# Gate products behind the next mixer tile, and the last sums of squares taken later, in a two-block transformer on one core

## The reference

```python
# second block; h: 1040 tokens (16 meta tokens ahead) x 1024
u = rmsnorm_2(h, g_pre_mix[l])
z = u @ w_in[l]                      # 512 q, 128 k, 128 v, 512 xr, 512 yr
...
xr = causal_depthwise_conv(xr, conv_w[l], conv_b[l])        # width 4
# rg_lru: block-diagonal gates, 8 blocks of 64
r = sigmoid(xb @ w_a + b_a);  i = sigmoid(xb @ w_x + b_x)
a = exp(-8 * r * softplus(-lam))
u = sqrt(-expm1(2 * log_a)) * (i * x)
h_t = a_t * h_(t-1) + u_t                                   # over the tokens
rec = gelu(yr) * hr
mix = concatenate([attn, rec]) @ w_out[l]
h = h + rmsnorm_2(mix, g_post_mix[l])
u = rmsnorm_2(h, g_pre_ffn[l])
f = square(relu(u @ w_ff1[l])) @ w_ff2[l]                   # 1024 -> 4096 -> 1024
h = h + rmsnorm_2(f, g_post_ffn[l])
return h[:, N_META:]
```

## Time and profile before

| | |
|---|---|
| device time, median of 3 runs | 2332.53 us (2332.31 to 2332.61) |
| device time of the profiled execution | 2331.14 us, its span 2329.0 us |
| mean granted PE clock of it | 0.953 |
| PE busy | 2198.0 us, 94% |
| DVE busy | 1763.4 us, 76% |
| ACT busy | 1131.9 us, 49% |
| POOL busy | 421.9 us, 18% |

### The profile page before, as it was taken

One profiled execution on the slowest core, in us unless ns is written; L12 is line 12 of the kernel. 1 busy time (PEld: TensorE's weight loads), 2 busy tenths in 40 slices (PEclk: granted clock), 3 DMA queues, 4 the chain that ended last, 5 costly groups with the idle time before them and its releaser, 6 DMA issues. The chain is left out here.

```text
span 2329.0 us, 31104 instructions
## 1 busy us (share of the span) xinstructions
PE 2198.0 (94%) x10909; PEld 1868.8 (80%) x10909; DVE 1763.4 (76%) x2938; ACT 1131.9 (49%) x1944; POOL 421.9 (18%) x417
## 2 busy tenths in 40 slices
PE   8989899998999999999999989899999999999996
PEld 5779888886877788888887979777878788888875
DVE  7699855565599987878788585573799977767897
ACT  5478655554353333335444563484563333554442
POOL 2123122213330122220001212103321122000002
PEclk9985599999999999999999999899999999999997
DMA  9025200005443333238531101002356445755422
GB/s 380 29 71 154 79 14 14 32 1 169 150 136 119 142 115 115 90 118 315 186 93 40 46 28 37 19 2 97 103 190 239 168 153 195 246 197 179 124 91 73
DMA packets 93098, 276.38 MB, mean 119 GB/s; under 512 B 11137, under 2 KB 15649, under 8 KB 89121
## 3 DMA queue, kind: packets, MB, share of 16 engines
q1 hardware_dynamic: 85472, 226.64, 29.3%
q10 hardware_dynamic: 7488, 47.98, 5.0%
HBM read 208.19 MB, written 66.39 MB: 118 GB/s over the span
## 5 line engine op out<-in xcount | busy, mean ns | idle before, releaser
L159 PE MATMUL banks<-f_hi,f_w_hi 128*128 128x512 f32 x608 | 237.8, 391 | 5.8 <-DVE f_w_lo L3914 4.4
L160 PE MATMUL banks<-f_lo,f_w_hi 128*128 128x512 f32 x608 | 237.3, 390 | 0.0
L161 PE MATMUL banks<-f_hi,f_w_lo 128*128 128x512 f32 x608 | 237.2, 390 | 0.0
L3442 ACT CAST f_w_hi<-f_raw 128x512 fp32r<-128x512 f32 x173 | 107.5, 622 | 255.3 <-PE banks L161 190.3
L2017 ACT CAST w_hi<-w_raw 128x512 fp32r<-128x512 f32 x152 | 93.8, 622 | 223.7 <-PE set L161 106.5
L159 PE MATMUL set<-gate_hi,w_hi 128*128 128x512 f32 x420 | 163.8, 390 | 1.2 <-DVE w_lo L2349 0.8
L161 PE MATMUL set<-gate_hi,w_lo 128*128 128x512 f32 x420 | 163.4, 389 | 0.0
L160 PE MATMUL set<-gate_lo,w_hi 128*128 128x512 f32 x420 | 163.4, 389 | 0.0
L159 PE MATMUL set<-b_hi,w_hi 128*128 128x512 f32 x384 | 150.3, 391 | 4.8 <-ACT work L2027 2.6
L3122 POOL TENSOR_TENSOR f_w_lo<-f_raw,f_w_hi 128x512 fp32r<-128x512 f32 x64 | 93.6, 1464 | 337.6 <-ACT f_w_hi L3442 337.6
L161 PE MATMUL set<-b_hi,w_lo 128*128 128x512 f32 x384 | 149.5, 389 | 0.0
(11 more groups left out here) (583 smaller groups left out, 6093.9 us busy)
## 6 DMA issues: line engine op xcount, KB each, us to landing
gates<-x ACTq DMA_DIRECT2D x25, 1536.0 KB, 6.0
w_raw<-in_w_ff SPq DMA_DIRECT2D x53, 512.0 KB, 3.7
gate_raw<-gates SPq DMA_DIRECT2D x105, 256.0 KB, 2.9
f_gate_raw<-gates SPq DMA_DIRECT2D x70, 256.0 KB, 2.8
ada<-in_ada_w SPq DMA_DIRECT2D x32, 512.0 KB, 3.5
f_raw<-in_f_w_v SPq DMA_DIRECT2D x26, 512.0 KB, 3.6
f_raw<-in_f_w_u SPq DMA_DIRECT2D x25, 512.0 KB, 3.8
down_raw<-in_w_ff SPq DMA_DIRECT2D x18, 512.0 KB, 5.1
```

The source lines that it names most:

```text
L159: nc.tensor.matmul(out, w_hi, x_hi, start=start, stop=False)
L160: nc.tensor.matmul(out, w_hi, x_lo, start=False, stop=False)
L161: return nc.tensor.matmul(out, w_lo, x_hi, start=False, stop=stop)
L3442: nc.scalar.copy(w_parts(n)[0][:, :], source(n)).then_inc(w_hi_s, 1)
```

## The change

It has three parts, all of them in the written-out lists of steps.

1. **Recurrent half.** PE takes mixer tile 4+t ahead of gate set t. `gated(t)` is cut into `gated_input(t)` and `factor(t)`, and DVE's list is written in a new order; the four `recurred` stand at its end. On ACT, `weights_mix(5)` stands ahead of `conv_hi(0)`, `weights_mix(6)` to `(9)` between `exp_tanh` and `mult_root`, and the four `gelu` behind the last `mult_root`.
2. **Up projection.** `early_out(15)` stands two squares and one cast earlier in ACT's list.
3. **End.** `y_sum` comes one tile later on DVE, `sum_y` two tiles later on PE. POOL adds the squares of tiles 0 to 3 of the last piece to one, in three adds ahead of its residual adds; `sum_last` is done for t = 0 (that sum), 4, 5, 6, 7, the first two of them between the last tiles of products. The last sums get places in two PSUM banks. `spread_y(0)` and `spread_y(1)` are later on PE, and DVE's `scale_y` follow them.

```diff
--- before.py
+++ after.py
@@ -1551,16 +1551,17 @@
                                "y_inverted", "y_spread", "y_scaled"))
+        end_paired = c.sem("end_paired")
...
-        y_spread_at = [up[1][:, 0, 0:512], up[1][:, 1, 0:256], out[0][:, 0, 0:256]]
+        y_spread_at = [up[1][:, 0, 0:512], up[0][:, 1, 0:256], out[0][:, 0, 0:256]]
         end_square = [(end_sq if t < HALF else end_more)[:, t % HALF * 256:(t % HALF + 1) * 256] for t in range(KT)]
-        y_total_at = [up[0][:, 1, 0:4], up[0][:, 1, 4:6],
-                      up[0][:, :, 8:9].rearrange("p a b -> p (a b)")]
+        y_total_at = [up[0][:, 1, 0:4], up[0][:, 1, 4:6]]
+        y_last_at = [up[0][:, 0, 8:9], up[1][:, 1, 256:257]]
...
@@ -1741,6 +1742,12 @@
                         weights_low(n)
+                pool.wait_ge(y_squared, 2 * KT + 2)
+                nc.gpsimd.tensor_tensor(end_square[0], end_square[0], end_square[1], ALU.add).then_inc(end_paired, 1)
+                pool.wait_ge(y_squared, 2 * KT + 4)
+                nc.gpsimd.tensor_tensor(end_square[2], end_square[2], end_square[3], ALU.add).then_inc(end_paired, 1)
+                pool.wait_ge(end_paired, 2)
+                nc.gpsimd.tensor_tensor(end_square[0], end_square[0], end_square[2], ALU.add).then_inc(end_paired, 1)
...
@@ -1897,9 +1904,12 @@
                 def sum_last(t):
-                    pe.wait_ge(y_squared, 2 * KT + t + 1)
+                    if t == 0:
+                        pe.wait_ge(end_paired, 3)
+                    else:
+                        pe.wait_ge(y_squared, 2 * KT + t + 1)
                     for j in range(2):
-                        mm = nc.tensor.matmul(y_total_at[2][:, j:j + 1], end_square[t][:, j * P:(j + 1) * P],
+                        mm = nc.tensor.matmul(y_last_at[j], end_square[t][:, j * P:(j + 1) * P],
...
@@ -1950,15 +1960,17 @@
                     for t in range(KT):
-                        if t == 3:
+                        if q == 2 and t == 4:
+                            spread_y(0)
+                        if t == 5:
                             sum_y(q - 1)
-                        if t == 7:
-                            spread_y(q - 1)
                         last_down(q, t)
-                pe.wait_ge(y_weighed, 2)
-                for t in range(KT):
+                        if q == 2 and t >= 6:
+                            sum_last(0 if t == 6 else HALF)
+                for t in range(HALF + 1, KT):
                     mm = sum_last(t)
                 mm.then_inc(y_total, 1)
+                spread_y(1)
...
@@ -2167,17 +2179,19 @@
                 early_out(13)
-                for k in range(4):
+                weights_high(17)
+                for k in range(2):
                     square_h(k)
-                weights_high(17)
                 early_out(14)
+                square_h(2)
+                early_out(15)
+                square_h(3)
+                weights_high(18)
                 for k in range(4, 6):
                     square_h(k)
-                weights_high(18)
-                early_out(15)
-                square_h(6)
                 weights_high(19)
-                square_h(7)
+                for k in range(6, 8):
+                    square_h(k)
...
@@ -2235,7 +2249,7 @@
                         y_square(q, t)
-                        if t == 4:
+                        if t == 6:
...
@@ -2612,6 +2626,13 @@
 
+                def weigh_last():
+                    dve.wait_ge(y_total, 3)
+                    for j in range(2):
+                        n = cols[2].start + j
+                        op = nc.vector.tensor_tensor(part[:, n:n + 1], y_last_at[j], scale2[:, n:n + 1], ALU.mult)
+                    op.then_inc(y_weighed, 1)
+
...
@@ -2625,33 +2646,32 @@
 
-                last_add(0, 0)
+                for q in range(2):
+                    for t in range(KT):
+                        last_add(q, t)
+                        if t > 1:
+                            y_sum(q, t - 1)
+                        elif t == 0 and q:
+                            y_sum(q - 1, KT - 1)
+                        if q and t == 6:
+                            weigh(0)
+                invert_y(0)
+                last_add(2, 0)
+                y_sum(1, KT - 1)
                 for t in range(1, KT):
-                    last_add(0, t)
-                    y_sum(0, t)
-                for t in range(KT):
-                    last_add(1, t)
-                    if t:
-                        y_sum(1, t)
-                    if t == 3:
-                        weigh(0)
-                    if t == 5:
-                        invert_y(0)
-                for t in range(KT):
                     last_add(2, t)
-                    if t == 3:
+                    if t == 6:
                         weigh(1)
-                    if t == 5:
-                        invert_y(1)
-                    if t % 2:
-                        scale_y(0, t // 2)
-                for k in range(HALF, KT):
+                    if t >= 4:
+                        scale_y(0, t - 4)
+                invert_y(1)
+                for k in range(4, 6):
                     scale_y(0, k)
-                weigh(2)
-                for k in range(HALF):
-                    scale_y(1, k)
+                weigh_last()
+                scale_y(0, 6)
+                scale_y(0, 7)
                 invert_y(2)
-                for k in range(HALF, KT):
+                for k in range(KT):
...
@@ -3404,8 +3424,8 @@
                 for t in range(LRU_T):
+                    mix_products(4 + t)
                     gates_of(t)
-                    mix_products(4 + t)
...
@@ -3769,33 +3789,30 @@
                 nc.scalar.activation(lam_t[3][:, :], lam_t[2][:, :], ACT.Ln, bias=1.0).then_inc(lam_act, 1)
+                weights_mix(5)
                 conv_hi(0)
-                weights_mix(5)
                 sigmoids(0)
                 conv_hi(1)
                 exp_tanh(0)
+                weights_mix(6)
                 mult_root(0)
-                weights_mix(6)
                 sigmoids(1)
                 conv_hi(2)
                 exp_tanh(1)
+                weights_mix(7)
                 mult_root(1)
-                weights_mix(7)
                 sigmoids(2)
                 conv_hi(3)
-                gelu(0)
                 exp_tanh(2)
+                weights_mix(8)
                 mult_root(2)
-                weights_mix(8)
                 sigmoids(3)
-                gelu(1)
                 exp_tanh(3)
+                weights_mix(9)
                 mult_root(3)
-                weights_mix(9)
-                gelu(2)
-                weights_mix(10)
-                gelu(3)
-                for n in (11, 12, 13):
+                for t in range(LRU_T):
+                    gelu(t)
+                for n in (10, 11, 12, 13):
...
@@ -4332,10 +4349,12 @@
 
-                def gated(t):
+                def gated_input(t):
                     dve.wait_ge(gate_free, 2 * CH2 * (t + 1))
                     nc.vector.tensor_tensor(lru.gi[:, :], lru.gi[:, :], lru.xc[t % 2][:, :], ALU.mult)\
                         .then_inc(gated_s, 1)
+
+                def factor(t):
...
@@ -4399,28 +4418,30 @@
                 evacuate(XR[3], work[:, 3, :]).then_inc(xr_used, 1)
+                gate_branch(0)
+                gated_input(0)
                 conv_lo(1)
+                factor(0)
                 rescale(2)
-                gated(0)
                 state(0)
                 convolve_2(2)
-                gate_branch(0)
                 conv_lo(2)
-                gated(1)
+                gated_input(1)
+                factor(1)
+                gate_branch(1)
                 state(1)
                 convolve_2(3)
-                gate_branch(1)
                 conv_lo(3)
-                gated(2)
+                gated_input(2)
+                factor(2)
+                gate_branch(2)
                 state(2)
-                gate_branch(2)
-                recurred(0)
-                gated(3)
+                gated_input(3)
+                factor(3)
+                gate_branch(3)
                 state(3)
-                recurred(1)
-                gate_branch(3)
-                recurred(2)
-                recurred(3)
+                for t in range(LRU_T):
+                    recurred(t)
...
```

## The result

| | before | changed |
|---|---|---|
| device time, median of 5 runs | 2332.61 us (2332.31 to 2333.53) | 2315.11 us (2311.85 to 2320.15) |
| ratio, 95% interval | | 0.9924 [0.9913, 0.9935] |
| span of the profiled execution | 2329.0 | 2313.3 |
| granted PE clock of it | 0.953 | 0.955 |

What follows compares the result with a forecast made beforehand. TensorE (PE), busy 94% of the span, was taken to bound the kernel. Terms of -9.9 (recurrent half), -1.2 (early copy) and -8.0 (end) sum to -19.1, from 2332.5 to 2313.4 us; range 2307 to 2321.

Steps and rivals of the forecast that it cites:

- -9.9: Recurrent half: one whole mixer tile moves into PE's waits, 1.7 us of it lost to a later last gate set.
- -1.2: Up projection: ACT's copy comes 1.7 us earlier, but a low part from DVE then comes 0.6 too late; 1.2 us gained.
- -8.0: End: DVE's last add 8.6 us earlier, its first final add waiting for POOL until 2312.6; DVE ends at 2318.9, not 2326.9.
- PE without a wait at set 0; tile 8 near 1404.7: Recurrent half: gate set 0 starts at 1348.1 without a wait; gate set 3 ends and mixer tile 8 starts near 1404.7.
- No wait at set 1: Recurrent half: a chain of 11.4 us from 1352.2 starts sigmoids 1 at 1363.6, when PE has just reached the set.
- Cycles of 18.5, the second product about 3.2: Recurrent half: state chain 18.5 us for tiles 2 and 3; DVE's second product of each tile about 3.2 beside POOL's subtraction.
- two cycles 1.95 shorter each: Bound for the recurrent half: if POOL never got ahead of DVE's second product, about -13.5 us.
- Waits of 3.5 and 2, and the clock at half in both: Recurrent half: PE waits some 3.5 us in gate set 2 and 2 in set 3, and the granted clock falls there.
- Rival (a): End: DVE is let in between POOL's instructions, end term -12.1, total -23.2, 2309.3 us; chance 0.15.
- (b): Recurrent half: the state chain sets it with its old longest cycle of 21.1, total -13.9, 2318.6 us; chance 0.15.
- (c): Recurrent half: PE loses in sets 2 and 3 what it saves at 0 and 1; total -9.2, 2323.3 us; chance 0.04.
- (d): PE's clock stays at 1.2 GHz through the tile behind sets 1, 2 and 3: +15.5, 2348.0 us; chance 0.03.

Runs made afterwards that it cites:

- later_gates: Changed kernel with gate sets 2 and 3 behind two mixer tiles each, DVE and ACT steps fitted, a one-column sigmoid behind each root: 2309.8 us, ratio 0.9897 to before.
- small_low: Changed kernel with POOL's subtraction for the low weights of mixer tiles 6 to 9 on 128 of 1024 columns: 2312.1 us, ratio 0.9899 to before.
- psum_inverse: Changed kernel with the inverse of the last piece in PSUM: 2317.4 us, ratio 0.9923 to before.
- psum_end: Changed kernel with the inverse of the last piece and the last eight scaled products in PSUM: 2315.8 us, ratio 0.9920 to before.

## Why the prediction was right

The forecast was 2313.4 against 2315.1, within its range. Its three terms were -9.9, -1.2 and -8.0. The recurrent half came as -10.5 in the first trace and as -8.0 to -9.5 in the seven other traces with the same half; the early copy gave nothing (M is 0.3 longer, and 0.2 to 0.5 at the place itself); the end came as -8.7. That the sum of the stretches, -18.9, is so near to -19.1 is in part luck: a larger end and a good draw of the clock in the half stand for the missing -1.2, and the 3.2 of the early part, which no term had, moved the span the other way.

- **PE without a wait at set 0; tile 8 near 1404.7.** Both so: 0.17, and 1404.5 on the scale of before.
- **No wait at set 1.** Wrong by 1.5. My chain from set 0 to sigmoids 1 had the table load follow the root; it waits for PE's first group of the set, 1.16 after the root's end. Sigmoids 1 started at 1368.26, not 1366.8 (1363.6 and the 3.2 by which this execution was late). With the load taken ahead in later_gates the wait was 0.45. The chain also left out `rescale(2)` and the product of the state, but that product ended at 1367.09, before the load was through, and cost nothing here.
- **Cycles of 18.5, the second product about 3.2.** 18.8 (root to root, 1364.73 to 1383.51) and 3.33. small_low shows the cause: with POOL's subtraction cut from 2.52 us to 0.59 the product is 1.39. The bound of "two cycles 1.95 shorter each" was right for the product; A became 1.9 to 4.3 us shorter than in the eight traces.
- **Waits of 3.5 and 2, and the clock at half in both.** 2.62 and 2.57, and behind which set the clock fell changed from one execution to the next, so A lies between 136.8 and 139.2 in eight traces of kernels that are the same in this half. The waits of sets 1 to 3 are 6.7 in sum where 5.5 was forecast, and the clock fell behind one of them instead of two; these errors offset each other in the first trace.
- **-1.2 for the early copy.** The term is wrong, by 1.2 and more. The wait became 1.7 shorter, and the three low parts behind it took back 1.3 (0.56 + 0.43 + 0.29), of which I had counted the first alone (0.6, it was 0.56). The rest went in the products between, in steps too small for the timeline to name: over the whole place it is 17.0 against 16.7.
- **-8.0 for the end.** The mechanism holds, its place was another. I had put POOL's backlog in front of the first final add (4.4 us); it came in front of the two-column product (3.25), then POOL ran dry for 0.49, and the adds got through at 0.69 and less. psum_inverse moves it back to where I had it, 5.31. The terms ahead are as worked out: last add after 14.5 (14.4 forecast). POOL ended 1.6 later than forecast. As forecast, PE stood at no sum of squares.
- Rival (a), DVE let in between POOL's adds, is half true: DVE came in at the next boundary where the operation took 0.94 and 0.69, and was kept out where it took 3.25 and 5.31. Rivals (b) and (c) didn't come, nor did (d), the slow clock through whole tiles: behind the waits of the changed kernel it lasted 3 to 7 us.

What stays open: why DVE comes in at one boundary of POOL's adds and is kept out over seven at another, what decides whether the clock falls behind a wait of 2.6 us, and whether the change shifts the start of the program.

## What to carry to other kernels

Put work that is independent in front of the step that waits, and list what sits in front of each link of the waiting chain on its own engine: here a table load behind a semaphore was worth 1.05 us of PE's wait at one set, and a POOL subtraction that a moved cast had released was worth 1.9 us of a DVE product per tile. When a wait is made shorter, list all the waits right behind it: three small ones took back 1.3 of 1.7 us here, and the place as a whole gained nothing. After shortening an engine's tail, look at the queue that stores its results; and judge a change of a few us by stretches between fixed instructions, since the same short idle time of PE was followed by no fall of the clock in two traces and by one that cost 2.9 us in two others.

## What the runs showed of the hardware that was not expected

- The Trainium skill, "SBUF — State Buffer", section "Who interferes with whom", has the port pair that VectorE and GpSimd share locked for a whole instruction by whoever issues first; I had read that as the waiting engine being let in when this instruction ends. The traces agree with that reading in part only: a DVE operation on two SBUF operands waited for one POOL instruction in the changed kernel (0.94), but through seven further ones in psum_inverse (5.31 us of an add of 0.42).
- With one operand in PSUM, DVE was not held up beside POOL's run, as psum_end's theory had it: its eight final adds took 0.42 each, six of them while POOL was adding, and the product of two columns took 0.16 instead of 3.25.
- A wait of 2.6 us of PE was followed by a clock of 1.00 in two traces and of 0.53 over seven us in two others, with the same instructions around it; the clocks of the two pairs had differed some 235 us earlier.
- An ACT table load can wait for a semaphore of the instruction it belongs to. In the changed kernel that of the sigmoids started 1.16 after the root had ended, with PE's first group of the set; with a one-column sigmoid ahead, PE's wait at set 1 was 0.45 instead of 1.50.
